# Low-rank products of an RWKV mixer contracted over 128 rows instead of 64, in a re-woven two-layer float32 kernel

## The reference, cut to what matters

```python
w_code = codes[..., : 2 * W_LORA].reshape(b, t, 2, W_LORA)      # W_LORA = A_LORA = 64
a_code = codes[..., 2 * W_LORA:].reshape(b, t, 2, A_LORA)
for d in range(2):
    w = w0[d] + jnp.tanh(w_code[:, :, d]) @ w_lora_b[d]
    decay = jnp.exp(-jnp.exp(-jax.nn.softplus(-w) - 0.5))
    a = jax.nn.sigmoid(a0[d] + a_code[:, :, d] @ a_lora_b[d])
    ...
    o = o + rwkv7_scan(hd(r), hd(decay), hd(k_d), hd(v), kk, hd(a), reverse=(d == 1))
```

## Time and profile before

| what | value |
|---|---|
| median of 3 runs | 3089.81 us (3079.1 to 3100.5) |
| profiled execution | 3096.89 us, of which span 3095.1 us |
| mean granted TensorE clock | 0.986 |
| PE busy | 3005.3 us, 97% of the span |
| DVE, ACT, POOL busy | 54%, 23%, 8% |

### The profile page before, as it was taken

One profiled execution on the slowest core, in us unless ns is written; L12 is line 12 of the kernel. 1 busy time (PEld: TensorE's weight loads), 2 busy tenths in 40 slices (PEclk: granted clock), 3 DMA queues, 4 the chain that ended last, 5 costly groups with the idle time before them and its releaser, 6 DMA issues.

```text
span 3095.1 us, 45126 instructions
## 1 busy us (share of the span) xinstructions
PE 3005.3 (97%) x18944; PEld 2479.6 (80%) x18944; DVE 1656.2 (54%) x3430; ACT 720.4 (23%) x1352; POOL 260.4 (8%) x326
## 2 busy tenths in 40 slices
PE   8999999999999999999999999899999999999999
PEld 7878878888886887878888888696769959766894
DVE  3565557644521455655754441475237757646675
ACT  2333424322211243342422320100111010013100
POOL 1120302101200021120200200000000000000000
PEclk9999999999999999999999999999999999999999
DMA  5332333333333323323333344445334545433443
GB/s 221 125 99 102 96 98 122 96 102 119 113 126 129 139 103 99 122 83 104 115 99 113 99 125 136 144 168 173 136 123 152 175 151 173 166 115 116 150 164 123
DMA packets 153754, 395.56 MB, mean 128 GB/s; under 512 B 90288, under 2 KB 106800, under 8 KB 109648
## 3 DMA queue, kind: packets, MB, share of 16 engines
q1 hardware_dynamic: 51376, 367.94, 34.3%
q10 hardware_dynamic: 100608, 19.93, 3.4%
q0 software_dynamic: 1568, 4.79, 0.4%
HBM read 380.04 MB, written 12.59 MB: 127 GB/s over the span
## 4 chain that ended last, share of the span: by engine, by line
PE 88%; DVE 6%; DMA 4%; ACT 1%; issue 1%; ACTq 0%; DVEq 0%; SPq 0%
PE bank L418 26%; PE bank L1975 18%; PE bank L1993 7%; PE bank L435 7%; PE bank L1798 7%; PE bank L1861 4%; PE bank L1404 2%; DMA rw_ex<-x_scratch 2%; PE bank L2004 1%; DMA x_scratch<-rw_ex 1%; PE bank L1686 1%; PE bank L772 1%; PE bank L752 1%; PE bank L910 1%; PE bank L895 1%; PE bank L991 1%
## 5 line engine op out<-in xcount | busy, mean ns | idle before, releaser
L418 PE MATMUL bank<-h_features,weight_ring 128*128 128x256 f32 x4192 | 963.1, 383 | 2.5 <-DVE h_features L531 1.0
L418 PEld LDWEIGHTS bank<-h_features,weight_ring 128*128 128x128 f32 x4192 | 780.4, 190 | 117.1 <-issue 10.9
L435 PE MATMUL bank<-weight_ring,h_features 128*128 128x256 f32 (+1 forms) x896 | 206.7, 381 | 2.8 <-ACT rt_qk L1703 2.7
L435 PEld LDWEIGHTS bank<-weight_ring,h_features 128*128 128x128 f32 x896 | 165.7, 192 | 28.8 <-ACT rt_qk L1703 3.9
L1975 PE MATMUL bank<-h_features,weight_ring 128*128 128x128 f32 x1408 | 172.0, 275 | 6.2 <-DVE h_features L531 6.2
L1975 PEld LDWEIGHTS bank<-h_features,weight_ring 128*128 128x128 f32 x1408 | 164.3, 192 | 6.9 <-DVE h_features L531 6.9
L2046 ACT COPY mem_normed<-bank 128x128 f32<-128x128 f32 x88 | 23.5, 267 | 481.9 <-PE bank L1975 476.2
L1798 PE MATMUL bank<-y_features,weight_ring 128*128 128x256 f32 x512 | 123.7, 393 | 0.0
L1798 PEld LDWEIGHTS bank<-y_features,weight_ring 128*128 128x128 f32 x512 | 98.0, 197 | 14.5 <-issue 1.3
L2131 DVE TENSOR_TENSOR mem_normed<-mem_normed,bank 128x256 f32<-128x256 f32 x88 | 37.1, 421 | 130.6 <-PE bank L1975 130.6
L1975 PE MATMUL bank<-h_features,y_features 128*128 128x128 f32 x704 | 93.0, 275 | 0.0
(11 more groups left out here) (544 smaller groups left out, 4952.8 us busy)
## 6 DMA issues: line engine op xcount, KB each, us to landing
weight_ring<-in_w_in SPq DMA_DIRECT2D x146, 1024.0 KB, 5.1
weight_ring<-in_f00w SPq DMA_DIRECT2D x33, 1024.0 KB, 4.9
weight_ring<-in_f01w SPq DMA_DIRECT2D x33, 1024.0 KB, 4.8
weight_ring<-in_f10w SPq DMA_DIRECT2D x33, 1024.0 KB, 4.8
weight_ring<-in_f11w SPq DMA_DIRECT2D x33, 1024.0 KB, 4.8
weight_ring<-in_w_b SPq DMA_DIRECT2D x16, 1024.0 KB, 4.9
weight_ring<-in_w_out SPq DMA_DIRECT2D x16, 1024.0 KB, 4.9
weight_ring<-in_conv_in SPq DMA_DIRECT2D x10, 1024.0 KB, 4.9
```

The source lines that it names most:

```text
L418: m = e.matmul(bank[:, j, :], w[:, k, j * P:(j + 1) * P], x[:, k, :], start=k == 0, stop=k == kt - 1, skip_group_check=True)
L435: m = e.matmul(bank[:, t * n:(t + 1) * n], x[:, k, t * P:(t + 1) * P], w[:, k, :], start=k == 0, stop=k == kt - 1, skip_group_check=True)
```

## The change

Each low-rank weight tile becomes two tiles, one for each direction, of 128 rows. All four are cleared once at the start of the program by POOL; after that each quarter loads only the 64 rows of its direction into each, so the other 64 rows stay zero. The matmuls contract all 128 rows of tile and codes; they are as many as before. POOL issues four loads of 64x256 a quarter instead of two of 128x256, and the first low-rank product of a quarter waits for one semaphore more. The rotary tile moves into the memory of the second block's tiles. The weave table has new strings for all five engines in both mixer layers; the letters' counts stay the same.

```diff
 ORDER = {
     ("mixers0", "tensor"):
         "R P4 R4 H P4 H2 P4 H2 P5 H P H P H5 P H P4 H3 R2 P R2 P R2 P R4 P H6 B P4 B R H R3 P R2 P R2 P R P2 R H2 "
-        "B R2 P B R3 P H2 B2 R P B R2 P R2 H2 R P R P R2 P R6 H2 B4 H2 B5 R2 B R2 H2 R2 B R4 H2 B10 H5 R4 B2 R2 "
+        "B R2 P B R3 P H2 B2 R P B R2 P R2 H2 R P R P R2 H2 R6 P B3 H2 B5 R2 H2 B R2 B R2 H2 R4 B2 H2 B4 H3 B4 R "
...
-    R.lora = [R("lora_w", 2 * P), R("lora_a", 2 * P)]
+    R.lora = [[R(f"lora_{n}{d}", 2 * P) for d in range(2)] for n in "wa"]
...
                 if d == 0 and code == 0:
-                    e.wait_ge(g.lora_sem, 32 * (4 * l + q + 1))
+                    e.wait_ge(g.lora_sem, 64 * (4 * l + q + 1))
+                    e.wait_ge(*g.st.pool.at("lora"))
                     e.wait_ge(*g.cd.act.at("tanh", l))
                 for n in range(2):
-                    m = e.matmul(bank[:, n, :], R.lora[code][d * 64:(d + 1) * 64, n * P:(n + 1) * P],
-                                 g.codes[d * 64:(d + 1) * 64, code, :], start=True, stop=True, skip_group_check=True)
+                    m = e.matmul(bank[:, n, :], R.lora[code][d][:, n * P:(n + 1) * P], g.codes[:, code, :],
+                                 start=True, stop=True, skip_group_check=True)
...
         for i, lora in enumerate(("lora_w", "lora_a")):
-            e.dma_start(R.lora[i], g.t[f"{lora}{l}"][:, 2 * q * P:2 * (q + 1) * P]).then_inc(g.lora_sem, 16)
+            for d, rows in enumerate(ROW_HALVES):
+                e.dma_start(R.lora[i][d][rows], g.t[f"{lora}{l}"][rows, 2 * q * P:2 * (q + 1) * P]).then_inc(
+                    g.lora_sem, 16)
...
     e.memset(g.nm_one, 1.0).then_inc(*g.st.pool.up("one"))
+    for z in (z for code in g.R.lora for z in code):
+        e.memset(z, 0.0).then_inc(*g.st.pool.up("lora"))
...
-        rope = sb("rope", 5 * TT * 32)[:, :]
...
+            rope = keep("rope", 5 * TT * 32)
```

More of the change, by code:

```diff
@@ L3101, in __init__ @@
         self.pos_i = sb("positions", TT, I32)[:, :]
-        rope = sb("rope", 5 * TT * 32)[:, :]
-        self.cos_t, self.sin_t, self.rope_ang, self.rope_n, self.rope_r = (
-            view(rope[:, i * 64:(i + 1) * 64], (TT, 32)) for i in range(5))
         with ExitStack() as stage:
@@ L3111, in __init__ @@
             self.act_t, self.silu = keep("act", FT, T), keep("silu", 2, T)
+            rope = keep("rope", 5 * TT * 32)
+            self.cos_t, self.sin_t, self.rope_ang, self.rope_n, self.rope_r = (
+                view(rope[:, i * 64:(i + 1) * 64], (TT, 32)) for i in range(5))
             self.final_gain = flat(self.act_t[:, 0:4, :])
```

## The result

The changed kernel takes 3104.81 us (median of 15 runs, 3092.0 to 3119.1), the kernel before 3089.42 us (15 runs beside them): ratio 1.0058, 95% interval 1.0043 to 1.0072, so some 18 us slower (the two medians alone differ by 15). The forecast was 3096 us, 7 us slower on its own sum. The profiled execution took 3113.86 us, 9 us over its kernel's median, as that of before lies 7 us over its own; the two profiles differ by 17 us.

What follows compares the result with a forecast made beforehand. It took PE, 88% of the chain, to bound the kernel, with waits and clock worth about 80 us. Terms -5 + 0 + 9 + 0 + 3 = +7 us on the 3089.81 us median gave 3096 us, range 3066 to 3120.

Steps and rivals of the forecast that it cites:

- within 1%: Whole kernel: a time less than 1% (31 us) from the kernel before, given a chance of 0.85.
- Part 1: Low-rank products on PE: contracting 128 rows saves 0.3 us in each of 16 groups, -5 us, between 0 and -7.
- Rival C: Low-rank products: 64-row groups cost nothing extra, 5 us more than forecast, 3101; counted inside the forecast's chance of 0.60.
- Part 2: Four low-rank loads a quarter for two: later landings covered by the new order, sum 0 us, +3 if loads land slowly.
- Part 3: Round trips of the inverse through DRAM under the new order: changed cover costs +9 us at `rw_ex`, between -4 and +18.
- My own sign of being wrong: Mixer layers: a wait in no row of before, such as ACT held by a gate, taking over 5 us per layer.
- Part 4: Remaining PE waits and PE's clock: other waits 0 within 6 us to each side, clock +3 us.
- Clock: PE's clock falls behind stalls; new and removed waits together cost +3 us, between -12 and +14.
- Rival A: Third and fourth units stop waiting and two clock falls go: -31 us, 3062 at its far end; chance 0.23.
- faster by over 1%: Whole kernel: a time below 3059 us, said to need more than Rival A; chance 0.06.
- Rival B: Fifth unit waits 6.6 us per layer with a 7 us clock fall behind each: +22 to +27, about 3117; chance 0.17.

Runs made afterwards that it cites:

- E10: Changed kernel with the old weave order and waits on SP's weight chunks in five units of each layer: 3038.6 us, 0.9831 to the kernel before.
- E9: Kernel before with only waits on SP's weight chunks added, in five units of each layer: 3047.8 us, 0.9859 to the kernel before.
- E1: Changed kernel with the old weave order put back: 3085.7 us, 0.9998 to the kernel before.
- E3: Kernel before with each of its two low-rank loads a quarter split in two of 64 rows: 1.0020 to the kernel before.
- E2: Changed kernel with 64-row products and two loads a quarter again, so the new weave order alone: 3110.6 us, 1.0088 to the kernel before.
- E5: Changed kernel with waits on SP's weight chunks at the fourth and sixth units of each layer: 3075.8 us, 0.9958 to the kernel before.
- E12: Changed kernel, new order kept, with waits on SP's weight chunks in seven units of each layer: 3056.1 us, 0.9900 to the kernel before.
- E11: E10 with the SP waits in all eight units of each layer: 0.9841 to the kernel before, 1.4 us over E10 by the medians.

## Why the prediction was right or wrong

The direction, the range and "within 1%" held. The size was 7 for 18 us, and that it came out this near is in part luck: the +9 us stood at a wait whose sum did not grow, and a wait that had no term brought +10. By its own terms:

**Part 1, -5 us: right.** At the first unit the group took 32.88 - 31.16 = 1.72 us, where it was 1.92:

```profile
31.16 1.03 PE L898 MATMUL bank<-codes,rw_lora_w 128*128 128x256 f32 x4
32.02 1.03 PE L898 MATMUL bank<-codes,rw_lora_a 128*128 128x256 f32 x4
32.88 3.40 PE L420 MATMUL bank<-h_features,weight_ring 128*128 128x256 f32 x15
```

Over all 16 groups of E10 it took 1.73 to 1.80 us against 1.89 to 1.92 in E9, and the four 128x256 matmuls behind it 1.73 us against 1.83. So 0.15 us in each of 16 groups, and 0.10 us behind each, are 4 us. The three pairs of kernels gave more: -7 us (E1 less E3), -9 (changed kernel less E2) and -9 (E10 less E9), the last two with the price of the four loads in them. The intervals are some 4 us on each ratio, so these do not contradict the 4 us of the rows. In the last pair 7 us less at the low clock explain 3 of it. The rule on the drain at a change of mode (the Trainium skill, TensorEngine Tiling (Array Packing), section Key Properties) agrees: both the group and its follower became shorter, by 0.25 us together. Rival C, that the 64-row groups cost nothing extra, is refuted by the rows of its groups.

**Part 2, 0 us: the fourth quarters as predicted (no wait), the third not.** "The wait ahead of L898 in the third quarters at 0.7 to 1.0 us" was 2.5 and 3.0. The failed step is the landing time: I took the median of 4.1 us, and in both third quarters the loads landed 5.8 to 6.3 us after their issue (4.2 before). The cover's growth was right: in the first layer, from POOL's first issue to the moment when PE had nothing left to do, it was 4.15 us before and 4.98 us after. The bound of 5.9 us was that of `lora_w` alone; the loads of `lora_a` landed in up to 6.6 us in the same trace. In the new order five weight chunks are issued around this place, two in the old. The four loads themselves are worth 1 us of it (E2), and +6 us for the whole kernel in E3, where I had given 0 with cover and +3 at the worst.

**Part 3, +9 us at `rw_ex`: wrong.** The waits there summed to 14.5 us in the whole run where they had been 15.8. The third unit, forecast 1.3 us later, had no wait in the first layer and 2.1 us in the second (4.1 before); the fifth, forecast with a new wait of 2 us, waited 0.41 and 0.61; the second, forecast unchanged, waited 6.29 us in the second layer (2.50 before): PE was there 1.8 us earlier, and the load landed 2.0 us later. The failed step is the first one: I took each unit's trip as a given length and changed only the cover. The length is not given. From the first store's issue to the last landing it is 7.6 to 9.6 us in the units that E5 and E10 gate, and 10.3 to 17.4 us in all 32 trips of the two kernels, each of which has at least one chunk of SP issued into it or just ahead. The new order moved the chunks: away from the third unit of the first layer, onto the `xT_scratch` transfer of the fourth and sixth. I wrote that the spread of 2.7 to 11.5 us was "the weak point of this count" and did not ask what made the spread; the rows of SP's queue stood in the trace of before. The transposed load had no term in the sum at all: it measured +10.4 us. My own sign of being wrong, a wait over 5 us in each layer that is in no row of before, came close to this: `rw_bm` took 8.4 and 5.3 us, and stood in the earlier trace rows with 1.7.

**Part 4, other waits 0 within 6 us: held.** L797 +5.0, L1423 +3.2 and L437 for `mixed_features` +2.1 came; the waits for `rt_qk` (2.7), `hg_ks` (1.9) and `hg_qs` (1.6) went. With the small ones it is about +4. **Clock, +3 us:** 68 us at the low level in the mixer layers of before (my 77 came from a mean rounded to 0.98), 82 after, so +7: inside the bounds of -12 and +14, and twice the term. The link to waits was right.

Set against the profiles' difference of 17 us: -4, +3 (L898), -1 (`rw_ex`), +10 (`rw_bm`), +4 (others), +7 (clock, all in the mixer layers) are 19; the records do not resolve the last 2.

**Rival A** had the right mechanism for two units: the waits of the third and fourth unit in the first layer went, and that of the fourth in the second. It missed that the transfers would be met elsewhere. Its far end was summed wrongly: -31 us from the median is 3059, not 3062, so "faster by over 1%" began at A's far end and not beyond it. **Rival B** asked for a late load in the fifth unit and a fall of the clock behind it. The kind of event was right and its place wrong: it happened at L765 in the fourth and sixth units of both layers. E5, which removes these four events, is 31 us faster, so 8 us each, where B had 13 for one. Last, the prediction took 1% for what a measurement can't resolve; 15 runs of each kernel resolved 18 us to within some 4 us.

## What to carry to other kernels

In this kernel a round trip through DRAM had no length of its own: some 8 us alone, up to 17 with weight loads in its way. Before its cover is counted, the transfers that are issued while it runs have to be read from the queues of the other engines; if large ones meet it and are not urgent, a wait on the engine that issues them is worth a try. Here it cost nothing (no wait for the weight ring came in E5 to E12, and E11's three more gates moved no more than 1.4 us) and gave back 1.4% of the time (E9), where the new order took 0.9% (E2). And a wait of PE is to be priced with the fall of the clock behind it: in E5 12.7 us of waits for `rw_bm` went and 31 us of time.

## What the hardware showed that I had not expected

- Two transfers of 128 KB on one queue, issued 2.2 us apart: 2.7 us for the first and 12.6 for the second, with three chunks of 1 MB issued from another queue at the second one's start. With the chunks held back (E5) all four landed in 2.8 to 3.7 us.
- How long the clock stayed low differed by the place of the wait and not by its length alone. In the changed kernel, behind the four waits of 2.2 to 3.0 us at L797 and L898, the low level lasted 3.4 us or did not come. At the four longer waits at L765 (1.9 to 4.7 us) it lasted 7 to 14 us, and at L754 10 us at the wait of 6.3 us and 14 us behind one of 1.5 us; small 64x32 matmuls follow there. But five other waits at L754, of 0.2 to 1.9 us, had no fall behind them, the one of 2.1 us had 3.4 us, and in the kernel before the two longest there (3.2 and 4.1 us) had 3.4 us. Whether these matmuls or the wait keep it low was not tried.
- The second block, which no kernel here alters, takes 1122 us from its wait of 7.1 us on in every trace but E12's (1135), with 16 to 20 us at the low level (49 in E12's). So the differences between the other profiles, E10's 58 us under the kernel before too, lie in the mixer layers.
